# Order of a step in the prompt latent attention: the projection of the next pair of heads before the transposes, its eviction before the probability copies

## The reference

```
k_nope = einsum('bsc,chd->bshd', ckv, w_uk)        # 8 heads of 64
v      = einsum('bsc,chd->bshd', ckv, w_uv)
sc = einsum('bqhd,bkhd->bhqk', qn, k_nope) + einsum('bqhr,bkr->bhqk', qr, kr)
p  = softmax(where(kpos <= qpos, sc * 96 ** -0.5, -inf))
o  = einsum('bhqk,bkhd->bqhd', p, v)               # blocks of 128 queries
```

## Time and profile before

| | us |
|---|---|
| median of 3 runs | 2671.6 (2671.32 to 2672.89) |
| the profiled execution | 2676.84 |
| its span, first to last instruction | 2674.8 |
| latent attention of the prompt in it | 1284 to 1477 |
| TensorE busy over the span | 2521.2 (94%) |
| VectorE, ScalarE busy over the span | 1049.7 (39%), 534.7 (20%) |
| mean granted clock of TensorE | 0.967 of full |

### The profile page before, as it was taken

How to read it: one execution, slowest core, us unless ns; L and a number is a source line. 1 busy time by engine, 2 the same in 40 slices (tenths; PEclk the granted TensorE clock), 3 DMA queues, 4 the chain that set the end, 5 groups by cost and what they waited for, 6 DMA issues and landing times.

```text
span 2674.8 us, 40337 instructions
## 1 busy us (share of the span) xinstructions
PE 2521.2 (94%) x16073; PEld 2387.7 (89%) x16073; DVE 1049.7 (39%) x1809; ACT 534.7 (20%) x1270; POOL 910.9 (34%) x468
## 2 busy tenths in 40 slices
PE   4999999999998999999998789799899999999996
PEld 3999999999987997999765668699799999999996
DVE  7222222222255564200566452674622222222226
ACT  3100000000022441211555332211300000000002
POOL 6333333333345341432000120344333333333332
PEclk9999999999999999999999886799899999999998
DMA  4222221212123232321212251562121211111111
GB/s 161 70 87 74 75 86 68 85 70 88 66 91 125 101 139 91 126 92 70 71 35 54 82 207 66 175 217 79 50 80 69 97 48 41 47 48 41 47 48 64
DMA packets 85167, 229.41 MB, mean 86 GB/s; under 512 B 8746, under 2 KB 47187, under 8 KB 83891
## 3 DMA queue, kind: packets, MB, share of 16 engines
q1 hardware_dynamic: 78922, 207.86, 22.3%
q10 hardware_dynamic: 6088, 19.23, 1.8%
HBM read 196.66 MB, written 74.39 MB: 101 GB/s over the span
## 4 chain that ended last, share of the span: by engine, by line
PE 52%; DVE 5%; issue 2%; DMA 1%; ACT 1%; POOL 1%; SPq 0%; DVEq 0%; ACTq 0%; POOLq 0%
PE ps L768 13%; PE ps L769 13%; PE ps L770 13%; PE ps L1001 2%; PE ps L1270 2%; PE ps L1016 1%; PE ps L1034 1%; PE ps L881 1%; PE ps L883 1%; PE ps L882 1%; DMA sgt<-scratch_gates 1%; PE ps L1235 1%; PE ps L1253 1%; PE ps L1215 1%; PE ps L1082 1%
## 5 line engine op out<-in xcount | busy, mean ns | idle before, releaser
L768 PE MATMUL ps<-u_hi,w_hi 128*128 128x352 f32 (+1 forms) x2880 | 931.4, 323 | 26.7 <-DVE u_lo L401 19.0
L769 PE MATMUL ps<-u_lo,w_hi 128*128 128x352 f32 (+1 forms) x2880 | 923.1, 321 | 0.0
L770 PE MATMUL ps<-u_hi,w_lo 128*128 128x352 f32 (+1 forms) x2880 | 920.9, 320 | 0.0
L679 POOL TENSOR_TENSOR w_hi<-raw,zero 128x1024 fp32r<-128x1024 f32 x184 | 352.0, 1913 | 1322.1 <-PE ps L768 1108.5
L768 PEld LDWEIGHTS ps<-u_hi,w_hi 128*128 128x128 f32 x2880 | 543.9, 189 | 40.3 <-DVE u_lo L401 19.6
L769 PEld LDWEIGHTS ps<-u_lo,w_hi 128*128 128x128 f32 x2880 | 544.6, 189 | 0.4 <-issue 0.2
L770 PEld LDWEIGHTS ps<-u_hi,w_lo 128*128 128x128 f32 x2880 | 543.8, 189 | 0.0
L682 POOL TENSOR_TENSOR w_lo<-raw,w_hi 128x1024 fp32r<-128x1024 f32 x184 | 450.5, 2448 | 14.5
L1803 DVE TENSOR_TENSOR h<-ps,silu 128x352 f32<-128x352 f32 x132 | 68.1, 516 | 750.2 <-PE ps L770 745.0
L768 PE MATMUL ps<-h_hi,w_hi 128*128 128x352 f32 (+1 forms) x1056 | 342.2, 324 | 12.4 <-DVE x L1812 10.0
L1812 DVE SCALAR_TENSOR_TENSOR x<-ps,x 128x352 f32<-128x352 f32 (+1 forms) x528 | 270.5, 515 | 209.1 <-PE ps L770 209.0
(11 more groups left out here) (261 smaller groups left out, 2579.4 us busy)
## 6 DMA issues: line engine op xcount, KB each, us to landing
raw<-in_wstream SPq DMA_DIRECT2D x186, 512.0 KB, 3.2
out_win_out<-in_cache_win SPq DMA_DIRECT2D x23, 1424.0 KB
latn<-in_cache_mla SPq DMA_DIRECT2D x128, 80.0 KB, 1.9
scratch_gates<-stage ACTq DMA_DIRECT2D x16, 516.0 KB, 2.6
out_win_out<-in_cache_win SPq DMA_DIRECT2D x7, 1168.0 KB
kv_d<-in_cache_win SPq DMA_DIRECT2D x24, 256.0 KB, 9.4
sgt<-scratch_gates SPq DMA_DIRECT2D x16, 352.0 KB, 3.9
scratch_x_mid<-x SPq DMA_DIRECT2D x1, 4128.0 KB, 13.0
```

The source lines that it names most:

```text
L679: nc.gpsimd.tensor_tensor(hi, raw[:, s % RAW], zero[:].to_broadcast([P, UW]), ALU.add).then_inc(w_hi_done, 1)
L768: a = mm(out, wh, xh, start=start, stop=False)
L769: mm(out, wh, xl, start=False, stop=False)
L770: return a, mm(out, wl, xh, start=False, stop=stop)
```

## The change

Two moves of calls, no instruction added or removed. On TensorE the projection piece of a step is issued before the transposes, that is right after the values, or after the scores where the step has no values. On ScalarE its eviction comes before the probability copies. VectorE's order stays.

```diff
@@ TensorE, in the loop over S @@
                 j, k, kbs = filler(S)
                 if k is not None:
                     values(k, kbs)
-                if S > 0:
-                    transposes(S - 1)
                 if j is not None:
                     pe.wait_ge(pj_act, pj_act_count(j - 1))
                     pe.wait_ge(pj_dve, pj_dve_count(j - 1))
                     projection(j, 7)
+                if S > 0:
+                    transposes(S - 1)
@@ ScalarE, in the loop over S @@
                 if S < N_MLA - 1:
                     exponential(S + 1)
-                if S > 0:
-                    copy_probs(S - 1)
                 j, _, _ = filler(S)
                 if j is not None:
                     projected(j)
+                if S > 0:
+                    copy_probs(S - 1)
                 if pv_ends(S) is not None:
                     keep_om(pv_ends(S))
```

## The result

The changed kernel takes 2684.0 us (median of 7 runs, 2681.17 to 2688.65), the kernel before beside it 2672.89 (7 runs, 2671.32 to 2678.9). The ratio is 1.004, with the interval 1.0028 to 1.0052: slower, by 7.5 to 13.9 us. The prediction had 2678.0 us and a range that ended at 2682.0. The direction was right, the time lies outside.

A forecast was written before the change was run, and what follows sets the result against it. TensorE was taken to bound the steps with projection pieces; added waits 2.01 + 2.08 + 2.08 plus 0.26 for restarts gave 6.4 us, so 2671.6 + 6.4 = 2678.0 us, own range 2675.0 to 2680.5, full range 2671.5 to 2682.0.

The forecast's parts named there:

- The bound and the loop: In the 30 steps with a projection piece: TensorE bounds; transposes release an exponential, ScalarE's other work queues behind; at most 2.6 us to win.
- The sum of the added waits: Latent attention: 2.01 us while pair 1 is made, 2.08 each for pairs 2 and 3, 0.26 for restarts; 6.4 us slower.
- The thirteen waits: Five, four and four new waits of TensorE for a piece's eviction, in the three stretches of steps with projection pieces.
- restarts: TensorE restarting after each of 13 waits, with a weight load covered before: 0.02 us each, 0.26 in all (0 to 1.3).
- 0.91 us for n = 2: Estimated time of TensorE's scores before the next piece, at about 0.22 us a block; subtracted in S = 21's wait of 0.51.
- S = 16 to 18: Wait in S = 17 shortened and more than paid back in S = 18, where a head output is kept: +0.19 us.
- Nothing gives it back: Steps after the stretches start from transposes on TensorE and move as a whole, so the 6.4 us stay.
- Rival 1: Lateness recovered in later steps where TensorE waits for ScalarE's copies: +0.6 to -0.7 us left, 2671.6 us; chance 0.10.
- rival 2: The move covers TensorE's three named waits and adds few: 2.6 us faster, 2669.0 us; chance 0.07.
- rival 4: TensorE's granted clock falls from 2.4 to 1.2 GHz in three steps: 8.4 us more, 2686.4 us; chance 0.04.
- Rival 3: Late exponentials delay the row maximum or eight-column copy; 13 waits grow by some 0.3 us: 10.3 us, 2681.9 us; chance 0.13.
- "some 15" waits: Sign of being right: TensorE waits for ScalarE some 15 times instead of three, 0.3 to 0.8 us, in steps without values.

The follow-up runs named there:

- e5: Changed kernel, with ScalarE evicting the piece before the exponential instead of after it; latent attention 178.4 us.
- e9: Changed kernel, with a kept head output taken by ScalarE before the exponential and by VectorE right after the row maximum; S = 18 shortens by 0.43 us.
- e6: Kernel before, with both moves only in the 13 steps that have values; latent attention 6.0 us more.
- e1: The kernel before built a second time without an edit; latent attention 177.06 us.
- e4: Kernel before with ScalarE's move alone, eviction ahead of the probability copies; stretches 31.9, 28.7 and 28.7 us.
- e3: Kernel before with TensorE's move alone, projection piece ahead of the transposes; latent attention 189.95 us.
- e12: Changed kernel, with kept head output and piece eviction before the exponential on ScalarE, right after the row maximum on VectorE; latent attention 170.8 us, ratio 0.9974.

## Why the prediction was right inside and wrong in its time

The steps of the stretches, start to start, in us, against what was forecast:

```
steps S    before   after   more   forecast
4 to 6      8.47     8.58   0.11   0
7           2.55     2.95   0.40   0.40
8           2.67     3.21   0.54   0.57
9           2.87     3.14   0.27   0.28
12          3.51     3.81   0.30   0.28
13          3.88     4.38   0.50   0.48
16 to 20   14.71    15.02   0.31   0.19
21          2.22     2.70   0.48   0.51
22          3.16     3.21   0.05   0
23          2.48     2.87   0.39   0.40
24          3.12     3.67   0.55   0.57
25          3.24     3.65   0.41   0.41
```

S = 10, 11, 14 and 15 are not in the table; they moved by 0.06 us or less. S = 32 to 41 repeat S = 16 to 25.

- *The bound and the loop* (transposes release an exponential, the eviction is queued behind it): right. e5 takes 5.1 of 6.5 us away by the eviction's place alone.
- *The sum of the added waits*, 2.01 + 2.08 + 2.08 + 0.26 = 6.4 us: right, 6.5 to 6.7 in three profiles, but its last term was made good by luck. The thirteen waits came to 5.7 us, against 5.8 by their terms without any restart, so the 0.26 us for restarts are not seen. Something of that size stands elsewhere: S = 16 to 20 have 0.31 instead of 0.19, S = 4 to 6 have 0.11 instead of 0, and moved steps with values in which nothing waits are 0.04 to 0.06 us longer (S = 10: 4.02 to 4.08; S = 20: 2.78 to 2.82), which the prediction had at 0. (Where the working gives 0.91 us for n = 2, the scores issued in S = 21 are those of S = 22, with n = 3; the sum is not touched.)
- *S = 16 to 18*: right in kind. S = 17 became shorter (2.32 to 2.17) and S = 18 paid more than that back (3.16 to 3.64), by the kept head output, as e9 shows.
- *Nothing gives it back*: right, S = 26 to 31 take 19.6 us before and 19.5 after, scores(43) to scores(63) 53.5 in both. Rival 1 is out. So are rival 2, and rival 4 (clock 1.00 in the stretches). Rival 3's extra is not there either.
- *"some 15" waits of 0.3 to 0.8 us*: too literal. Eleven are named, of 0.2 to 1.3 us. The others are in the starts alone.
- **The step that failed** is the last one: "It lies 5.2 us above the median of the runs, and so the median becomes 2671.6 + 6.4 = 2678.0 us". It took the three runs, 2671.32 to 2672.89, for the level and the spread of the kernel. In 106 runs that kernel has the mean 2675.8 and spans 2669.5 to 2681.9; only 23 of them lie at 2672.89 or below, and all three of mine were among the low ones. From 2675.8 the same sum gives 2682.2, and the 23 runs of the changed kernel have 2683.5. The profiled execution, 2676.84, was the better anchor, and I moved away from it. With it goes the statement that 0.2% (5.3 us) is about what a measurement can tell from no change: the intervals here, with 6 to 12 runs against 26 or 31, reach 2 to 4 us to either side, while a median of three can miss the level by 4 us. That the changed kernel's first seven runs had 2684.0, and not 2682.2, is within that scatter.

What stays open: 7.6 us (6.3 to 9.0) in the runs against 6.5 to 6.7 in the profiles. And over all kernels the total follows the latent attention only to some 4 us: e6 has 6.0 us more there, and its ratio gives 2.1 (-0.8 to 5.1). Behind scores(63) the profiles take 1204.0 to 1211.5 us for the same instructions. Nearly all of that spread is in the sample tokens' stage and the dilated attention: from VectorE's first instruction there (L1980 in the kernel before) to its L2216 it is 241.5 us in e6 and 249.4 in e1. The changed kernel alone has 248.8, 243.2 and 243.8 in its three profiles, the kernel before 248.8 and 249.4, so in the first comparison this part was equal. Whether a program also has a level of its own there, by the moment at which the stage starts, these runs do not settle.

## What to carry to other kernels

When independent work is moved on TensorE ahead of the instruction that releases another engine, that engine's whole queue is late by the moved piece (here 6.5 us of 177 with both moves, 12.9 with TensorE's alone); so look first at what stands in that queue behind the released instruction, above all the eviction that the moved work itself needs. On an engine that stands waiting for a release, put the evictions whose data are there already ahead of the wait, not behind it. And where a forecast is some 0.3% of the time, take the level from as many runs as there are and the change from stage lengths in the profile: here the stage's length repeated to 0.2 us, while the totals of one kernel spread over 12.

## What the runs showed of the hardware

**The total.** One program's executions spread over 12 us of 2676 (106 runs). Inside the latent attention two profiles of the kernel before agree to 0.01 us over 177, and three of the changed kernel to 0.2 over 184. The granted clock there was the same in all of them: 0.83 to 0.84 between 1290 and 1300 us, which holds a short time at the lower level, and full behind it. Ahead of it, in a stage where TensorE is busy 66 to 69 us of 80, it was 0.94 and 0.89 in the two profiles of the kernel before and 0.87, 0.89 and 0.89 in the three of the changed one. The Trainium skill ("TensorE: Matmul & The Clock Gate", "What's actually happening") says that the window by which the gate judges activity runs freely and does not start anew with a kernel, so that the moment at which the clock changes varies. Clocks that differ between executions of one program fit that; no run here shows their cause.

**VectorE beside GpSimd.** A scaling of 128x896 on VectorE takes 0.69 us alone and up to 2.24 us while GpSimd splits weights (e4), and ends 0.47 to 0.48 us after GpSimd's instruction in six profiles. A stage's length can depend in this way on when a transfer lands: S = 29 took 4.59 us in e4, and 3.92 or less in the other thirteen profiles.

**Order alone.** With the same instructions and only their order changed, the latent attention took between 189.95 us (e3) and 170.81 (e12).
